# A transformer kernel in one stream of weights: attentions and the recurrent branch set beside the next branch's projections, and the modulation matmuls set between the weight pieces of a merge

## The reference, cut to what matters

```
h  = rms(x);  proj(name) = h @ w_in[:, cols(name)]
y_fox = attention(rms(q), rms(k), v, decay from fox_f)         # 16 heads of 64, causal
y_lru = scan(conv(lru_x), gates r and i by block matmuls) * gelu(lru_g)
y_sb  = stick_breaking_attention(sb_q, sb_k, sb_v)             # 16 heads of 64
y_mem = attention(rms(mem_q), rms(mem_n @ w_k), mem_n @ w_v)   # 4 heads of 256
x = x + sum_n(sigmoid(proj(gates)_n + b_n) * (y_n @ w_branch_n)) @ w_out
x = x + (silu(conv(h2 @ w_gate)) * (h2 @ w_val)) @ w_down
```

```
mod = silu([c, c_ctx]) @ w_ada[layer] + b_ada[layer]     # 2 x 1024 by 1024 x 6144, per layer
h = rms(x) * g1 * (1 + scale) + shift; x = x + gate * merged; ...
```

## Time and profile before

| | us |
|---|---|
| median of 3 runs | 3234.0 (3230.39 to 3244.86) |
| profiled execution, its own time | 3241.71 |
| span of that execution | 3239.9 |
| busy PE, DVE, ACT in it | 2658.2, 1169.5, 882.3 |
| first block up to its merge | 531.3 |
| merge of the first block, to the output product | 194.2 |
| feed-forward part and layer 0 up to its experts | 978.5 |
| experts of layer 0, of layer 1 | 546.0, 516.9 |

### The profile page before, as it was taken

How to read it: one execution, slowest core, us unless ns; L and a number is a source line. 1 busy time by engine, 2 the same in 40 slices (tenths; PEclk the granted TensorE clock), 3 DMA queues, 4 the chain that set the end, 5 groups by cost and what they waited for, 6 DMA issues and landing times. The chain is left out here.

```text
span 3239.9 us, 36546 instructions
## 1 busy us (share of the span) xinstructions
PE 2658.2 (82%) x14364; PEld 1796.3 (55%) x14364; DVE 1169.5 (36%) x1596; ACT 882.3 (27%) x1314; POOL 39.9 (1%) x36
## 2 busy tenths in 40 slices
PE   6887898998998787889977778887887896787876
PEld 5666687998996464668753222223664894222222
DVE  4446544655753334344432001103444552000001
ACT  3344433544442232322221000002233432000001
POOL 0100000000000000000000000000000001000000
PEclk8888998999998898889978999998897997999999
DMA  4463532453542333112215999996211343999996
GB/s 154 157 257 113 198 130 92 178 185 123 188 159 91 150 136 130 50 69 100 85 46 224 404 405 407 403 414 260 78 52 50 142 165 147 413 410 409 411 410 269
DMA packets 92935, 669.19 MB, mean 207 GB/s; under 512 B 10320, under 2 KB 10496, under 8 KB 12800
## 3 DMA queue, kind: packets, MB, share of 16 engines
q1 hardware_dynamic: 90256, 654.67, 51.6%
q0 software_dynamic: 2272, 11.52, 1.0%
q10 hardware_dynamic: 272, 1.05, 0.1%
HBM read 666.13 MB, written 1.06 MB: 206 GB/s over the span
## 5 line engine op out<-in xcount | busy, mean ns | idle before, releaser
L1860 PE MATMUL ps<-ring,WK 128*64 128x512 f32 x3072 | 731.0, 605 | 171.2 <-DMA ring<-in_stream 147.1
L424 PE MATMUL ps<-A,piece_hi 128*128 128x256 f32 (+1 forms) x1952 | 618.5, 317 | 97.7 <-DVEq L358 33.1
L376 DVE TENSOR_TENSOR ring_lo<-ring,piece_hi 128x1024 fp32r<-128x1024 f32 x378 | 459.3, 1220 | 450.4 <-ACT piece_hi L369 449.3
L425 PE MATMUL ps<-A,piece_hi 128*128 128x256 f32 (+1 forms) x1952 | 612.5, 314 | 0.0
L426 PE MATMUL ps<-A,ring_lo 128*128 128x256 f32 (+1 forms) x1952 | 611.7, 313 | 0.0
L1860 PEld LDWEIGHTS ps<-ring,WK 128*64 128x64 f32 x3072 | 194.5, 137 | 674.2 <-DMA ring<-in_stream 371.9
L424 PEld LDWEIGHTS ps<-A,piece_hi 128*128 128x128 f32 x1952 | 384.7, 197 | 129.3 <-issue 59.2
L369 ACT ACTIVATE piece_hi<-ring 128x1024 fp32r<-128x1024 f32 x378 | 388.2, 1053 | 223.8 <-DVEq L450 131.9
L425 PEld LDWEIGHTS ps<-A,piece_hi 128*128 128x128 f32 x1952 | 385.6, 198 | 17.2
L426 PEld LDWEIGHTS ps<-A,ring_lo 128*128 128x128 f32 x1952 | 384.9, 197 | 18.1
L1980 DVE TENSOR_TENSOR WK<-WK,ps 128x512 f32<-128x512 f32 x32 | 22.0, 688 | 636.7 <-PE ps L1860 636.7
(11 more groups left out here) (252 smaller groups left out, 2447.6 us busy)
## 6 DMA issues: line engine op xcount, KB each, us to landing
ring<-in_stream SPq DMA_DIRECT2D x621, 1024.0 KB, 7.7
WK<-in_na_bias POOLq DMA_DIRECT2D x2, 2048.0 KB, 7.8
WK<-cum_scratch POOLq DMA_DIRECT2D x1, 2048.0 KB, 9.7
const<-in_const SPq DMA_DIRECT2D x1, 1267.0 KB, 11.7
WK<-in_x SPq DMA_DIRECT2D x1, 1024.0 KB, 5.4
WK<-in_mem SPq DMA_DIRECT2D x1, 1024.0 KB, 9.1
WK<-cum_scratch POOLq DMA_DIRECT2D x1, 1024.0 KB, 14.9
WK<-in_lru_w POOLq DMA_DIRECT2D x1, 1024.0 KB, 5.1
```

The lines of the kernel that those rows point to most:

```text
L376: nc.vector.tensor_tensor(ring_lo[:, slot, at:at + PIECE], ring[:, slot, at:at + PIECE], f32(piece_hi[:, j, :]), ALU.subtract).then_inc(lo ...
L424: nc.tensor.matmul(out_, l[0], r[0], start=first, stop=False)
L425: nc.tensor.matmul(out_, l[0], r[1], start=False, stop=False)
L1860: last = nc.tensor.matmul(ps[64 * n:64 * n + 64, bank, :], lhs, piece[:, n * 512:n * 512 + 512], start=(k == 0), stop=(k == DC - 1))
```

## The change

It has five parts.

1. In the fox attention each of the eight rounds now also does two of the 16 projection pieces of the recurrent branch: one between turn and product, one behind the product. They go to PSUM banks 6 and 7; the product moves from bank 6 to bank 4.
2. In the stage behind it the 24 pieces of the stick-breaking q, k, v are interleaved with the recurrent branch's convolution, gates, arithmetic and scan. That branch's buffers move (`LX` to `YT`, `LG` to `XT`, `LA` to `YT`).
3. The stick-breaking attention does two of the 16 pieces of the memory attention's k and q in each round.
4. The table `ADA` is gone. The 48 modulation steps stand in two merges: 32 in the first block's merge, a step behind every two split pieces, and 16 in the merge of the second block's layer 0. The stream is reordered to match: slot of split pieces, slot of modulation, slot of split pieces, and so on.
5. The first block's merge is written out instead of looped (`merge_loop` is gone), and banks are handed out from a ring that each stage chooses (`set_ring`), in the two merges with modulation six banks of eight.

```diff
-RAW_BEFORE = np.concatenate([[0], np.cumsum(RAW)])
+ADA_GROUPS = {0: ((0, 0), (0, 1), (0, 2), (1, 0)), 1: ((1, 1), (1, 2))}
+def ada_step(merge, slot):
+    return (*ADA_GROUPS[merge][slot // DC], slot % DC) if slot < DC * len(ADA_GROUPS[merge]) else None
...
+        def split_ahead(eng, cur):
+            while True:
+                while RAW[cur.s] and cur.s < PIECES:
+                    cur.s += 1
+                if cur.s >= PIECES or SPLIT_NO[cur.s] >= SPLIT_NO[cur.p] + AHEAD or cur.s > cur.p + 2 * R - 2:
+                    return
+                if cur.who == "act":
+                    split_hi(eng, cur)
...
         def next_piece(eng, cur, n=1):
             for _ in range(n):
+                assert RAW[cur.p] == SPLIT
                 cur.p += 1
-                if RAW[cur.s]:
-                    cur.s += 1
-                    continue
...
+                while RAW[cur.p] == ADA:
+                    cur.p += 1
+                split_ahead(eng, cur)
...
             for r in range(HEADS // 2):
-                if r + 2 < HEADS // 2:
-                    scores(r + 2)
                 turn(r)
+                also(2 * r)
                 product(r)
-                after(r)
+                also(2 * r + 1)
+                if r + 2 < HEADS // 2:
+                    scores(r + 2)
...
+            maxima(0)
+            probs(0)
             for r in range(HEADS // 2):
                 if r + 1 < HEADS // 2:
                     maxima(r + 1)
-                probs(r)
-                after(r)
+                also(2 * r)
+                if r + 1 < HEADS // 2:
+                    probs(r + 1)
+                also(2 * r + 1)
...
         def lru_pe(pe, cur):
-            pe.wait_ge(loads, 16 * LOADS["lru_w"])
-            for c in range(DC):
-                pe.wait_ge(lru_xc, c + 1)
-                bank_parts(pe, cur, [(P, g * T, T, [(LW[:, g, c, :], LXC[:, c, :])]) for g in range(2)])
+            for i in range(24):
+                sb_piece_pe(pe, cur, i)
+                if i < DC:
+                    if i == 0:
+                        pe.wait_ge(loads, 16 * LOADS["lru_w"])
+                    pe.wait_ge(lru_xc, i + 1)
+                    bank_parts(pe, cur, [(P, g * T, T, [(LW[:, g, i, :], LXC[:, i, :])]) for g in range(2)])
...
             for r in range(SB_ROUNDS):
                 turn(r)
+                mem_piece_pe(pe, cur, 2 * r)
+                product(r)
+                mem_piece_pe(pe, cur, 2 * r + 1)
                 if r + 2 < SB_ROUNDS:
                     scores(r + 2)
-                product(r)
-                after(r)
...
+            def two_pieces(moving, kc):
+                nonlocal slot
+                fm_banks(pe, cur, moving, n, 2 * DC // kc, kc)
+                if ada is not None:
+                    ada_pe(pe, cur, ada, slot)
+                slot += 1
...
-            merge_pe(pe, cur, 4, DC, T)
+            cur.set_ring(range(6))
+            merge_pe(pe, cur, 4, DC, T, ada=0)
+            cur.set_ring(range(NB))
```

More of the change, by code:

```diff
@@ L136, in __init__ @@
         self.g = 0
+        self.places = []
+        self.ring = list(range(NB))
+        self.turn = 0
+        self.uses = [0] * NB
         self.i = None
@@ new lines, in sb_piece_read, with op @@
+        def sb_piece_read(eng, who, cur, i):
+            if i < 2 * DC:
+                dst, scale = ((QT, HD ** -0.5), (KT, 1.0))[i // DC]
+                copies(eng, who, cur, lambda j: dst[:, j, :], 1, T, scale, first=i % DC)
+            elif i % 4 < 3:
+                next_piece(eng, cur)
+            else:
+                h = (i - 2 * DC) // 4
+                for j in range(TT):
+                    def op(bank, j=j):
+                        to = VT[:, j, h * 512:(h + 1) * 512]
+                        if who == "act":
+                            return nc.scalar.activation(to, bank, ACT.Copy)
+                        return nc.vector.tensor_copy(to, bank)
+                    read_bank(eng, cur, who == ("act", "dve")[j], op, piece=(j == TT - 1))
@@ L1286, in lru_dve @@
-            steps(nc.vector.tensor_tensor(LY, LXC[:, :, :], LG[:, :, :], ALU.mult))
-        def merge_loop(eng, cur, branches, kc, one_branch, steps=None, per=0):
-            if 2 * (4 + kc // 2) % (2 * R) == 0:
-                with loop(eng, cur, branches, pieces=2 * (4 + kc // 2), banks=16, steps=steps, steps_per=per) as i:
-                    one_branch(i)
-            else:
-                for i in range(branches):
-                    one_branch(i)
+            flat = lambda x: x.rearrange("p a t -> p (a t)")
@@ L1315, in merge_act @@
             yh, _ = y_split(kc, n)
-            def one_branch(i):
+            for i in range(branches):
                 for h in range(2):
@@ L1350, in one_branch @@
                         read_bank(dve, cur, True, op, piece=(kc == DC or j % 2 == 1))
+                        if (j + 1) * kc % (2 * DC) == 0:
+                            behind_two()
                     dve.drain().then_inc(gate_used, 1)
-            merge_loop(dve, cur, branches, kc, one_branch, steps=steps, per=8)
+            if ada is not None:
+                ada_dve(dve, cur, ada, slot)
             cur.add("merge", 2 * branches)
@@ L2108, in _ @@
                 barrier(pe, cur)
[L2109 removed]
+                att_pe(pe, cur, da_x)
                 barrier(pe, cur)
@@ L2200, in _ @@
                 barrier(act, cur)
-                att_act(act, cur, steps, da_x, **({"after": ada_with_act(act, cur, "da_x")} if layer == 0 else {}))
+                att_act(act, cur, steps, da_x)
                 barrier(act, cur)
@@ L2429, in fm, with ada @@
         put(w.reshape(P, w.shape[1], -1, P).transpose(0, 2, 1, 3))
-    def ada(l, *groups):
-        w = _rows(x["w_ada_2"][l])
-        for g in groups:
-            put(w[:, :, 2048 * g:2048 * (g + 1)])
+    def ada(merge, slot):
+        step = ada_step(merge, slot)
+        if step:
+            l, g, k = step
+            put(_rows(x["w_ada_2"][l][128 * k:128 * k + 128, 2048 * g:2048 * g + 2048]))
     w_in = x["w_in"][0]
```

580 lines of the change are left out of this document (316 added, 264 removed).

## The result

The changed kernel takes **3216.1 us** (median of 7 runs, 3212.8 to 3222.8) against 3234.0 before: ratio 0.9948, 95% interval 0.9928 to 0.9967. That is half a per cent faster where I forecast 3256, slower. The time lies inside the range that I gave (3212 to 3305), at its lower end; the direction is the wrong one, and so is what I said of the merge. The profiled execution has a span of 3211.1 us against 3239.9, 28.8 less. The forecast was 22 more; so 51 us are to be found.

The account below looks back on a forecast made before the run. PE, busy 82%, had holes for the change to fill, but ring slots would bound the first merge. -73 + 104 - 9 = +22 on the profiled 3241.7 gave 3264, or 3256 us from the median 3234.0; range 3212 to 3305.

Parts of the forecast that it names:

- First block up to the merge: All first-block stages ahead of its merge: overlapping projection pieces with attentions and recurrent branch saves 73 us.
- Fox attention: First block's fox attention with recurrent projections: 82.4 us against 115.5, rounds 9.2 apart, chained through DVE and ACT; -33.
- Recurrent branch: First block's recurrent branch interleaved with q, k, v pieces: 81.5 us against 102.8; -21.
- Stick-breaking: First block's stick-breaking attention with memory projections: PE bounds rounds of 9.0 us; 80.5 us against 99.3, -19.
- First merge: First block's merge with 32 modulation steps: ring slots, not PE, bound it; 299 us against 194.2, +104.
- the chain from signal to signal: First block's merge, freeing signal to next: issue, landing 4.8, splits, bank reads; 7.4 us where ACT reads, 9.6 where DVE.
- My halves of 35.5 and 38.1: First block's merge, us per half branch of four slots; the second also has the copy to ROWS and y's rounding.
- Second block: `na_x` -11.4, `da_x` -7, `na_ctx` -8 without steps; layer 0's merge +17 for 16 steps and two turns; sum -9.
- (a): First block's merge: ring deep enough, PE bounds it; +35 in place of +104, kernel 3187 us; chance 0.13.
- (b): Both attentions: ACT and DVE hold turns back 3 us per round over 16 rounds, +48, kernel 3304 us; chance 0.08.
- (c): First block's merge: chain holds for DVE's slots only, gates run at PE's 6.75; 21 us less, kernel 3235; chance 0.16.
- (d): First block's merge: PE's gaps of 2.8 us bring the lower clock; 387 in place of 299, kernel 3344; chance 0.05.

## Why the prediction was wrong, step by step

**First block up to the merge, -73: right** (-73.9), and the sum better than its parts: -35.3 for -33, -17.1 for -21, -18.7 for -19, and 2.8 from stages that I had left at nothing. That they cancel is luck. Fox attention: 80.2 for 82.4. The rounds are chained through ACT and DVE as said, 8.9 us apart for 9.2, with PE waiting 0.4 in each:

```profile
168.47 0.88 PE L1081 MATMUL ps<-const,WK 128*128 128x128 f32 x6
...
177.38 0.87 PE L1081 MATMUL ps<-const,WK 128*128 128x128 f32 x6 [0.45 <-DVE WK L1150]
...
186.28 0.88 PE L1081 MATMUL ps<-const,WK 128*128 128x128 f32 x6 [0.44 <-DVE WK L1150]
```

Recurrent branch: 85.7 for 81.5; three gate banks waited for the convolution (2.6 in all), one for the landing of `lru_w` (1.6), and the barrier's wait is 1.8. Stick-breaking: 80.6 for 80.5. Of the 2.8 us, 2.4 came from the memory attention.

**First merge, +104: wrong, +56.** The term that failed is the chain from signal to signal, in the sentence that what follows the split "stands in order behind it and ahead of the next signal". The last split of each period isn't ahead of it, nor, for gates, ACT's. So 7.8 stands for 9.6, 7.6 for 8.9 and 5.8 for 7.4, which puts the gates' interval under PE's 6.9; the short interval also lets the ring catch up, so 14 of the 32 pairs wait, each for 0.2 to 1.3. The 250 are made up like this: 32 pairs with their steps at PE's own 6.94 are 222, the waits for split pieces 9, three turns between branches with the slower pair behind each 11, the last turn and the end 8. My halves of 35.5 and 38.1 were 29 without the turns. The structure of the chain (ring of two, landing 4.8, DVE's reads the slower) was right: with the signal held back the merge takes 304, and a half of its pairs 35.6.

A size was off too: a step lengthens a pair by 1.17 (6.94 from pair to pair, 5.77 without steps), not by its own 0.96. And the mark that I had set for being wrong, a merge under 250, was set too low: 250.3 passes it while the mechanism had failed.

**Second block, -9: its sign right, too much by 5** (-3.8, of which a part may be spread). `na_x` lost 7.0 for 11.4, since layer 0's isn't layer 1's without steps (57.6 for 53.2); `na_ctx` lost 7.8 for 8, `da_x` 9.0 for 7; the merge gained 21.3 for 17: there PE has no gap, and a step lengthens a pair by 1.23 (12.11 for 10.88) where I had 0.96, a turn by 0.8.

**The rivals.** (a) would have needed the ring to be free of charge: PE is busy 228.9 of 250.3, 91%, and without the modulation's loads the merge takes 231.0. (b) fell: the rounds are as forecast. (c), gates at PE's pace, is what happened for the gates; its 3235 kept the wrong 9.6 for DVE's slots. (d) fell: the clock in the merge is 0.99, and the gaps at split pieces are at most 1.3 us and not 2.8. Only behind the turns, where PE had waited 1.5 to 1.9, did a pair take 6.7 to 6.9 us in place of 6.0. In the run with the signal held back the gaps do reach 3.5, and the busy time of the same matmuls rises from 228.9 to 247.5.

**What I took too lightly:** that the old fox attention carried its steps for nothing. The sum was not hurt, since the stage stood there as a whole, but it hid from me that the steps had a price of 27 us there, and so how much of the change was a move of cost from one place to another.

## What to carry to other kernels

When a chain runs through a buffer that is given back, ask which unit gives it back. Here an increment that stood by itself in DVE's list left before the operation ahead of it had begun, and one on a drain left 0.24 behind that operation's end; the merge took 261 us with the one and 304 with the other. Such an increment says nothing of the work ahead of it, so look at what it protects. And the signal belongs with whoever is idle at that moment: with ACT in DVE's place the merge was 7.5 us shorter in the profiled executions, with the same splits and reads.

## What the runs showed of the hardware

- A load is issued 0.12 us *before* the start of the DVE operation that stands ahead of its signal, 0.24 behind its end when a drain holds the signal.
- A drain that orders nothing adds 0.17 to DVE's order (1.31 for 1.14 from a split's start to the next read). The 64 of them made the merge 11 us longer, 8.1 of it as PE's busy time at a lower clock.
- With two loads issued side by side, the first still landed in 4.6 to 4.9 in the eight slots from 463.7 to 514.9 us; over the 64 loads of the merge the range is 4.6 to 8.8, median 5.6, at a DMA share of 0.72.
- PE with gaps of up to 1.3 us ahead of a pair took 6.0 us for it; in the run with gaps of 1.9 to 3.5 the mean clock of the merge was 0.91 in place of 0.99, and pairs behind them mostly took 7.5, though behind gaps of 1.98 and 2.13 a pair took 6.0.
- A modulation step, 0.96 us of PE's time in the old attentions, lengthens a pair of pieces by 1.17 (256 columns) and by 1.23 (512).
